# Memory attention: where VectorE empties the bank of a finished query projection

## The reference, cut to what matters

```
def memory_cross_attention(q_in, m_in, w_q, w_kv, w_o):
    q = (q_in @ w_q).reshape(bsz, s, XATTN_HEADS, XATTN_HEAD_DIM)
    k, v = jnp.split(m_in @ w_kv, 2, axis=-1)
    ...
    scores = jnp.einsum("bshd,bmhd->bhsm", q, k)
    probs = jax.nn.softmax(scores * (XATTN_HEAD_DIM ** -0.5), axis=-1)
    o = jnp.einsum("bhsm,bmhd->bshd", probs, v).reshape(bsz, s, D_MODEL)
    return o @ w_o
```

## Time and profile before

| | us |
|---|---|
| median of the three timed runs | 2298.84 |
| the three runs | 2298.84, 2299.88, 2294.38 |
| the profiled execution | 2296.93 |
| its span | 2295.1 |
| PE busy in it | 2223.7 |
| DVE busy in it | 1273.0 |
| mean granted TensorE clock | 0.983 of full |

### The profile page before, as it was taken

How to read it: one execution, slowest core, us unless ns; L and a number is a source line. 1 busy time by engine, 2 the same in 40 slices (tenths; PEclk the granted TensorE clock), 3 DMA queues, 4 the chain that set the end, 5 groups by cost and what they waited for, 6 DMA issues and landing times.

```text
span 2295.1 us, 28261 instructions
## 1 busy us (share of the span) xinstructions
PE 2223.7 (97%) x11052; PEld 1773.5 (77%) x11052; DVE 1273.0 (55%) x1994; ACT 865.2 (38%) x1458; POOL 326.7 (14%) x324
## 2 busy tenths in 40 slices
PE   8899999999999999999999999999989999999998
PEld 6778788778888887876678888887875558888887
DVE  5765566554444445266645455455578874555554
ACT  4433454434222224355543222233245653222223
POOL 1300351001000003032210000001045641000001
PEclk9999999999999999999999999999988999999999
DMA  5233114413333332311123333333230003333331
GB/s 162 75 105 89 47 50 125 120 38 100 96 97 93 100 92 83 92 47 47 38 74 100 94 96 98 97 96 101 92 92 1 2 12 92 100 95 99 93 100 46
DMA packets 292660, 187.80 MB, mean 82 GB/s; under 512 B 7856, under 2 KB 286768, under 8 KB 292528
## 3 DMA queue, kind: packets, MB, share of 16 engines
q1 hardware_dynamic: 292240, 185.78, 27.1%
q10 hardware_dynamic: 288, 0.21, 0.0%
HBM read 183.88 MB, written 2.10 MB: 81 GB/s over the span
## 4 chain that ended last, share of the span: by engine, by line
PE 78%; DVE 3%; ACT 1%; issue 1%; POOL 0%; ACTq 0%; DVEq 0%; POOLq 0%
PE ps L469 76%; PE ps L503 2%; DVE tmp L2374 0%; DVE sb_small L2680 0%; DVE nk_kwl L2407 0%; ACT ne_t L2631 0%; DVE sq L2375 0%; POOL acc L559 0%; DVE sb_small L2683 0%; DVE sq L612 0%; ACT wh L455 0%; ACT tmp L2631 0%; DVE st_L L2132 0%; DVE wl L465 0%; DVE XL L496 0%
## 5 line engine op out<-in xcount | busy, mean ns | idle before, releaser
L465 DVE TENSOR_TENSOR wl<-raw,wh 128x1024 fp32r<-128x1024 f32 x336 | 414.6, 1235 | 676.8 <-ACT wh L455 676.7
L455 ACT CAST wh<-raw 128x1024 fp32r<-128x1024 f32 x336 | 349.0, 1039 | 653.0 <-PE ps L469 637.5
L469 PE MATMUL ps<-xb_x,wh 128*128 128x512 f32 (+1 forms) x1488 | 462.2, 392 | 4.7 <-DVE sq L612 4.6
L469 PE MATMUL ps<-XH,wh 128*128 128x512 f32 x872 | 348.2, 399 | 10.4 <-issue 4.0
L469 PE MATMUL ps<-XH,wl 128*128 128x512 f32 x872 | 342.4, 393 | 0.0
L469 PE MATMUL ps<-XL,wh 128*128 128x512 f32 x872 | 342.1, 392 | 0.0
L469 PEld LDWEIGHTS ps<-xb_x,wh 128*128 128x128 f32 (+1 forms) x1488 | 277.2, 187 | 65.2 <-DVE sq L612 5.7
L469 PE MATMUL ps<-xb_x,wl 128*128 128x512 f32 (+1 forms) x744 | 291.9, 392 | 0.0
L559 POOL TENSOR_TENSOR acc<-acc,sq 128x512 f32<-128x512 f32 x55 | 76.1, 1383 | 1336.1 <-ACT sq L546 1334.8
L469 PEld LDWEIGHTS ps<-XH,wh 128*128 128x128 f32 x872 | 165.3, 190 | 47.5 <-issue 8.9
L469 PEld LDWEIGHTS ps<-XH,wl 128*128 128x128 f32 x872 | 165.2, 189 | 35.7
(11 more groups left out here) (365 smaller groups left out, 3549.2 us busy)
## 6 DMA issues: line engine op xcount, KB each, us to landing
raw<-in_mlp_w SPq DMA_DIRECT2D x128, 512.0 KB, 3.8
raw<-in_w_gate_up SPq DMA_DIRECT2D x44, 512.0 KB, 3.7
raw<-in_w_in SPq DMA_DIRECT2D x29, 512.0 KB, 3.7
raw<-in_sb_w_qkv SPq DMA_DIRECT2D x24, 512.0 KB, 3.7
raw<-in_w_down SPq DMA_DIRECT2D x22, 512.0 KB, 3.3
raw<-in_w_out_mix SPq DMA_DIRECT2D x16, 512.0 KB, 3.8
raw<-in_w_kv SPq DMA_DIRECT2D x16, 512.0 KB, 3.7
raw<-in_nsa_w_kv SPq DMA_DIRECT2D x12, 512.0 KB, 3.4
```

The costliest lines, as they stand in the source:

```text
L455: e.copy(shaped(WH[i % NH], i), shaped(RAW[i % NR], i)).then_inc(*w_hi.up(i))
L465: e.tensor_tensor(shaped(WL[i % NH], i), shaped(RAW[i % NR], i), shaped(WH[i % NH], i).bitcast(F), ALU.subtract).then_inc(*w_lo.up(i))
L469: return e.matmul(out, a, b, start=start, stop=stop, skip_group_check=True)
```

## The change

The eviction of a query block moves from the head of the odd step to the even step before it, between the scaling of the probabilities and the low part of the transposed probabilities. `half` is 1 in even steps, and `u` is the block whose second half TensorE does in that step; `u` is None from step 11 on. `left` in step n + 1 is the same block as `u` in step n, so the same six evictions are made, each once. Nothing else is moved: the block's high part on ScalarE and its low part on VectorE stay in the odd step.

```diff
         for n in range(-1, 21):
             u, half = xq_of(n)
             left = 1 + (n + 1) // 2 if n % 2 and 1 <= n <= 11 else None
-            if left is not None:
-                dve_xattn_q(e, left)
             if 0 <= n < 16:
                 t, w = got(("xs", n)), take(e, ("xm", n))
                 e.wait_ge(*scored.at("xs", n))
@@
                 e.tensor_scalar(pt[:, 0:ML], pt[:, 0:ML], w[:, 3:4], None, ALU.mult).then_inc(*v_made.up("xp", b))
+            if half and u is not None:
+                dve_xattn_q(e, u)
             if 2 <= n < 18:
                 b = n - 2
                 P_ = got(("xpts", b // 4))
```

## The result

The changed kernel has a median of 2290.93 us (2289.14 to 2292.10, six runs) against 2298.95 us (2294.38 to 2299.88, six runs); ratio 0.9967 with a 95% interval of 0.9954 to 0.9980. Five more rounds gave 2290.71 against 2298.58 us, ratio 0.9970 (0.9959 to 0.9981). That is 8 us between medians both times. Between means it is 7.6 us in the first runs (2290.85 and 2298.42) and 6.8 us in the five rounds (2290.88 and 2297.68). The profiled execution took 2290.94 us.

The account below looks back on a forecast made before the run. TensorE was taken as the bound, busy 2223.7 of 2295.1 us; four shortened stops, 2.9 + 2.3 = 5.2 us, gave 2293.6 from the median or 2292.3 from the mean, so 2292.7 us was predicted, range 2288.3 to 2297.5.

Parts of the forecast that it names:

- The bank wait: Steps 3, 5, 7 and 9: TensorE's stops for evictions of blocks 3 to 6 vanish, 2.9 + 2.3 = 5.2 us.
- The two lags: Eviction starts 0.43 us after the projection's last matmul starts; TensorE's next matmul starts 0.75 us after the eviction's start.
- The new wait on VectorE: The waiting eviction ends its wait before `xp_l` behind it could start (442.89 against 443.52); costed at nothing.
- What is late next: Step 4's scores need block 3's low part; margin falls from 0.79 to 0.29 us but holds, loss at most 0.5.
- that rival: Block 3's low part late in step 4, VectorE holding TensorE in step 10 or 11: gain 3.5 us, 2294.4; chance 0.15.
- The clock: Full clock from 440 to 480 us, so removed stops bring no clock gain; the 1.7 us lost near 490 stays.
- the stretch of rows 7: Half-speed stretch at 489 to 494 us, granted clock 0.66, 1.7 us of full-speed work lost; forecast to stay.
- the rival in which the stretch goes: Half-speed stretch at 490 us, or one in 1700 to 1750, not granted: gain 6.9 us, 2291.0; chance 0.17.
- The other side: Shifted gaps bring new half-speed stretches in the second model part, 1.7 us each, four giving 2299.5; chance 0.05.
- No effect: Something else, weights or `six` banks, holds TensorE in the odd steps; time stays, taken as 2297.9 us; chance 0.04.
- no stop of this loop costs clock: Between 440 and 480 us the granted clock is 1.00, so the loop's stops were said to cost no clock today.

Follow-up runs that it names:

- e2: Only the evictions of blocks 3, 4 and 5 made early, against the kernel before; median 2295.58 us, ratio 0.9991.
- e3: Only the eviction of block 6 made early, against the kernel before; median 2294.70 us, ratio 0.9987.
- e4: Kernel before with its old order, but query blocks alternate between two PSUM banks; median 2291.37 us, ratio 0.9967.
- e5: Changed kernel with needless matmuls filling the former stops in steps 3, 5, 7 and 9; median 2297.50 us, ratio 1.0005 to the kernel before.
- e6: Kernel before with each eviction moved later, behind the maximum and scaling of its odd step; median 2301.14 us, ratio 1.0016.
- e8: The kernel before again, unedited, one execution for a second trace; 2299.58 us.
- e7: Changed kernel plus alternating query banks, spare banks for scores 14 and transposes 12, output low parts moved to step 13; 2290.92 us, ratio 0.9971 to the kernel before.
- e10: Changed kernel plus eight needless matmuls ahead of the query block in step 9; median 2294.22 us, ratio 0.9985 to the kernel before.
- e11: Changed kernel plus four needless matmuls ahead of the query block in step 9; median 2290.90 us, ratio 0.9974 to the kernel before.
- e12: Kernel of e7 plus six needless matmuls in step 9; median 2293.55 us, ratio 0.9980 to the kernel before.
- e9: Kernel of e7 with scores 15 given the same spare bank as scores 14; median 2292.92 us, ratio 0.9978 to the kernel before.

## Why the prediction was right, and where it was off

**The bank wait, right in place and size.** Forecast: four stops, 5.2 us. Trace: 4.94 us. e2 and e3 share it nearly as forecast (2.6 and 2.2 for 2.9 and 2.3), e4 takes away the bank wait by other means with the same effect, e5 puts the time back, and e6 prolongs the stops and loses 3.5 us. The two lags, 0.43 and 0.75 us, held in step 3 to the hundredth (443.64 + 0.61 is 444.25). In steps 5, 7 and 9 the first was 0.50 us (468.49 to 468.99 in step 9), and TensorE, whose scores would have let it go on at 469.54 + 0.12 = 469.66, went on at 469.74. From the last query matmul of one block to the first of the next it takes 1.18 us in step 3 and 1.25 in steps 5, 7 and 9, where it took 2.13 three times and 3.49. That gives 0.95, 0.88, 0.88 and 2.24 us, and is the whole difference between 5.2 and 4.94. Why the eviction starts 0.07 us later in three of the four isn't shown.

**The new wait on VectorE, right.** I argued that nothing ready stands behind the waiting eviction, because the transposes come behind the projection on TensorE. `xp_l` starts 0.03 us after `xp_h` ends (444.12 against 444.09), and the maximum of step 3 at 444.46 on a clock 0.61 us late, 443.85 for the 443.9 forecast. By the queue rule that I cited from the Trainium skill ("TensorE: Matmul & The Clock Gate", section "Architectural detail: the array is 16× 32×32, not 1× 128×128"), a waiting head holds all behind it. The traces agree from both sides: before, the eviction that was ready stood behind the waiting `xp_l` and cost TensorE 0.81 us; after, the waiting eviction has nothing ready behind it and costs nothing.

**What is late next, right.** The margin of block 3's low part was to fall from 0.79 to 0.29 us; it fell to 0.28. The other half of that rival, a longer step 10 or 11, didn't come either: from TensorE's resumption in step 9 to its last query matmul it is 6.32 us (469.74 to 476.06) and was 6.33 (474.06 to 480.39).

**The clock, the step that was off.** I left the stretch of rows 7 in place and gave its disappearance a chance of 0.17 as a rival, at 1.7 us. It is gone in both traces after, and a second one, which I didn't list, is half as long. The size was wrong as well: the two give 0.8 and 0.9 us, not 1.7 and 3.4, since part of the time at half speed is time in which TensorE waits anyway. Near 490 us the waits show it: in the loop TensorE waits 1.0 us for the softmax's `tmp` in the five traces that have the stretch, and 1.6 to 1.7 us in all nine that lack it. Over the 24 runs of before that slope shows too: a mean clock lower by 0.004 is 9.2 us of full-speed work not granted, and the runs differ by 4.1 us (e8). So 5.2 us forecast became 6.8 between means (standard error 0.7; in the trace 4.9 for the stops and 1.6 for the clock), and 8 between medians, the median of before lying 0.9 us above its mean. I forecast "within 0.3%" with 0.71; the ratio is 0.9967 and 0.9970, just beyond that line and at it. The time, 2290.93, is 1.8 us below the 2292.7 forecast and inside the range. It all but meets the 2291.0 of the rival in which the stretch goes, but that rival had one stretch at 1.7 us where it was two at 0.8 and 0.9; the agreement is luck.

**The other side.** That clock can be lost far behind the edit is real in the traces: e7 lost 0.8 of its 1.2 us that way, e10 and e11 1.3 us each near 1144 us. In the means of their runs it isn't clear of the scatter. For the change itself it went the other way. Whether this is a property of the shift by 5 us or of the order I can't say; all twelve runs of the changed kernel have a mean clock of 0.983 to 0.986, 0.9845 on average, against 0.9826 before.

**No effect** is excluded by the ratio's interval. Its time was forecast as 2297.9 (2292.7 + 5.2), while the range, meant to reach up to it, ended at 2297.5; and the lower end, 2288.3, was counted from 2296.93, while the forecast of 2292.7 less two stretches is 2289.3. Neither slip decides anything here.

## What to carry to other kernels

Where two engines hand a single bank back and forth, put the instruction that frees the bank directly behind the work that it waits for, if all that it overtakes waits for something later on the same engine; then an in-order queue loses nothing. A second bank does the same without any order. And count a saving of a few microseconds in the trace by the same instructions in both kernels: stretches of lower clock outside the edit, which differ between executions of one kernel, can change the total by 1 to 2 us.

## What the runs showed of the hardware that I hadn't expected

What a half-speed stretch costs depends on where it falls. One of 3.4 us cost about 0.8 us near 490 us, where TensorE also waits for others, and 1.6 us at 475.5 us in e8, where it doesn't. Nor did the pauses near 490 us foretell the stretch there. TensorE worked without a pause from 440 to 480 us in e5 and had the stretch afterwards, as before the change with its four pauses. In every trace stops of 2 us or more in sum come right ahead of that place, in the changed kernel as well (0.33, 1.11 and 0.70 us between 482 and 486 us), which keeps full clock. The traces in which the stretch is absent are the two of the change, e3, e4, e6, e7, e10, e11 and e12; it is there in both traces of the kernel before, in e2, e5 and e9.

Inside the loop it is less plain than the prediction had it. The sentence that no stop of this loop costs clock rests on one trace. Four traces have the long stop of step 9: two of them have a half-speed stretch that begins near its end (at 475.5 us for 475.15 in e8, at 477.2 for 478.00 in e6), and two, the first trace of before and e2, don't. None of the ten traces in which that stop is absent or filled has one there. Whether the stop brings it isn't shown: e5, with the stops filled, was no faster than the kernel before. The Trainium skill ("TensorE: Matmul & The Clock Gate", section "A second HAM failure mode: psum-queue depth-cycling") reports a kernel in which short idles between groups in PSUM banks make the clock swing. Here the clock from 440 to 480 us was 1.00 in one trace and 0.96 in another of the same kernel with the same four pauses, so these runs neither bear the remark out nor refute it.
